# Activations and shared buffers of a two-block transformer kernel moved to multiples of 128 bytes in SBUF

## What is computed

```python
def first_block(x, ...):
    for i in range(2):
        hn = rms_norm(x, norm_mix[i])
        x = x + (even_mixer(hn, ...) if i % 2 == 0 else odd_mixer(hn, ...))
        x = x + sqrelu_mlp(rms_norm(x, norm_mlp[i]), mlp_w1[i], mlp_w2[i])
    return rms_norm(x, norm_final)

def second_block(x, ...):
    h = rms_norm_2(x, mix_norm_pre[layer])
    proj = jnp.einsum("bsd,de->bse", h, w_in[layer])
    ...
    up = jnp.einsum("bsd,df->bsf", rms_norm_2(x, ffn_norm_pre[layer]), w_up[layer])
    ...
    ffn_out = jnp.einsum("bsf,fd->bsd", jax.nn.gelu(gate) * val, w_down[layer])
    return x + rms_norm_2(ffn_out, ffn_norm_post[layer])
```

## The kernel before

| tensor | address before | modulo 128 |
|---|---|---|
| raw, w_lo | 16,512 | 0 |
| w_hi | 57,472 | 0 |
| bias | 98,432 | 0 |
| x | 114,880 | 64 |
| ident, ones | 123,072 and 123,584 | 64 |
| eps_ones | 130,272 | 96 |
| act_hi | 132,800 | 64 |
| act_lo | 140,992 | 64 |
| tmp0 region | 149,184 | 64 |
| arena region | 157,376 | 64 |

## Time and profile before

### The profile page before, as it was taken

How to read it: one execution, slowest core, us unless ns; L and a number is a source line. 1 busy time by engine, 2 the same in 40 slices (tenths; PEclk the granted TensorE clock), 3 DMA queues, 4 the chain that set the end, 5 groups by cost and what they waited for, 6 DMA issues and landing times.

```text
span 1220.7 us, 21634 instructions
## 1 busy us (share of the span) xinstructions
PE 1155.7 (95%) x9407; PEld 1111.2 (91%) x9407; DVE 794.5 (65%) x1131; ACT 587.8 (48%) x824; POOL 147.3 (12%) x83
## 2 busy tenths in 40 slices
PE   6899899999999999999999999999977979999997
PEld 5898679999998999999999989999975879999997
DVE  5647548775546565877543978875554678888842
ACT  4257645444334555444334465663354446665531
POOL 3000012000220003000022201400050030111000
PEclk9699799999999999999999999999988999999999
DMA  9733125655654544565565362555941444566550
GB/s 279 202 114 124 40 66 177 186 194 177 200 177 141 168 141 139 173 190 190 179 200 175 97 210 70 173 161 182 314 137 35 138 139 139 176 198 197 193 187 35
DMA packets 198770, 195.71 MB, mean 160 GB/s; under 512 B 9691, under 2 KB 196756, under 8 KB 198676
## 3 DMA queue, kind: packets, MB, share of 16 engines
q1 hardware_dynamic: 191360, 188.43, 48.6%
q10 hardware_dynamic: 7316, 5.91, 1.9%
HBM read 192.86 MB, written 1.46 MB: 159 GB/s over the span
## 4 chain that ended last, share of the span: by engine, by line
PE 79%; DVE 10%; DMA 3%; ACT 3%; POOL 2%; issue 2%; ACTq 1%; DVEq 0%; POOLq 0%
PE ps_gemm L1561 70%; PE ps_score L1628 2%; PE ps_out L1655 2%; DVE w_lo L1023 2%; PE ps_trans L1640 2%; DMA f_bias<-cum_scr 2%; PE ps_score L1850 2%; DVE prob L1063 1%; POOL f_bias L642 1%; DVE xc L1334 1%; DVE prob L1092 1%; ACTq L778 1%; PE ps_gemm L1726 1%; DVE rs L1035 1%; ACTq L765 1%
## 5 line engine op out<-in xcount | busy, mean ns | idle before, releaser
L1561 PE MATMUL ps_gemm<-act_hi,w_hi 128*128 128x256 f32 x1640 | 463.3, 284 | 19.1 <-ACT act_hi L957 6.7
L1561 PE MATMUL ps_gemm<-act_hi,w_lo 128*128 128x256 f32 x1640 | 458.3, 281 | 0.0
L1561 PE MATMUL ps_gemm<-act_lo,w_hi 128*128 128x256 f32 x1640 | 446.3, 281 | 0.0
L1023 DVE TENSOR_TENSOR w_lo<-raw,w_hi 128x2048 fp32r<-128x2048 f32 (+2 forms) x179 | 408.4, 2290 | 51.4 <-ACT w_hi L683 51.1
L683 ACT ACTIVATE w_hi<-raw 128x2048 fp32r<-128x2048 f32 (+2 forms) x179 | 332.6, 1862 | 187.6 <-DMA raw<-in_mlp_w 97.1
L1561 PEld LDWEIGHTS ps_gemm<-act_hi,w_hi 128*128 128x128 f32 x1640 | 311.2, 190 | 27.6 <-issue 17.5
L1561 PEld LDWEIGHTS ps_gemm<-act_hi,w_lo 128*128 128x128 f32 x1640 | 310.8, 190 | 0.2
L1561 PEld LDWEIGHTS ps_gemm<-act_lo,w_hi 128*128 128x128 f32 x1640 | 302.6, 188 | 1.5
L1561 PE MATMUL ps_gemm<-hid_lo,w_hi 128*128 128x256 f32 x512 | 143.1, 280 | 0.0
L1561 PE MATMUL ps_gemm<-hid_hi,w_lo 128*128 128x256 f32 x512 | 143.1, 280 | 0.0
L1561 PE MATMUL ps_gemm<-hid_hi,w_hi 128*128 128x256 f32 x512 | 142.8, 279 | 0.0
(11 more groups left out here) (282 smaller groups left out, 1733.4 us busy)
## 6 DMA issues: line engine op xcount, KB each, us to landing
raw<-in_mlp_w SPq DMA_DIRECT2D x64, 1024.0 KB, 5.3
raw<-in_w_in SPq DMA_DIRECT2D x30, 1024.0 KB, 5.5
raw<-in_w_up SPq DMA_DIRECT2D x24, 1024.0 KB, 5.3
raw<-in_od_w_in SPq DMA_DIRECT2D x12, 1024.0 KB, 5.1
raw<-in_w_down SPq DMA_DIRECT2D x12, 1024.0 KB, 5.3
raw<-in_ev_w_in SPq DMA_DIRECT2D x9, 1024.0 KB, 6.2
raw<-in_w_proj_a SPq DMA_DIRECT2D x8, 640.0 KB, 4.3
raw<-in_ev_w_out SPq DMA_DIRECT2D x4, 1024.0 KB, 5.5
```

The costliest lines, as they stand in the source:

```text
L1023: dve.tensor_tensor(w_lo[:, slot, 0:k, 0:n], raw[:, slot, 0:k, 0:n], w_hi[:, slot, 0:k, 0:n].bitcast(F32), ALU.subtract).then_inc(w_ready, 1)
L1561: ins = pe.matmul(dst, lhs, rhs, start=(first and opens and i == 0), stop=(last and closes and i + 1 == len(order)), skip_group_check=True)
```

## The change

Two numbers in `build`: `top[0]` is moved on by 64 bytes ahead of `act_hi`, and `tmp0` by a further 128, so everything from `tmp0` on lies 192 bytes further.

```diff
@@ -178,9 +178,10 @@
     rs_o = place("ffn_rs", [P, TB])
     fcq = place("f_cum_q", [P, TB, 16])
     fw = place("conv_f", [P, 4, 2 * NH2])
+    top[0] += 64
     act_hi = place("act_hi", [P, NX, T], F32R)
     act_lo = place("act_lo", [P, NX, T], F32R)
-    tmp0 = top[0]
+    tmp0 = top[0] + 128
     arena = tmp0 + 8 * K
     assert arena + 70 * K <= 229344, arena + 70 * K
```

## The result

The change made the kernel slower by 1.3%: 1,234.9 us (four executions, 1,233.4 to 1,239.8) against 1,220.4 (1,215.6 to 1,222.2) for the kernel before on the same chip, a ratio of 1.0128 with a 95% interval of 1.0102 to 1.0153. The profiled execution took 1,235.1 us, its span 1,233.3. The prediction, no change, was wrong, and the time lies above its range.

A forecast was written before the change was run, and what follows sets the result against it. TensorE, busy 95% of the span, was taken to bound the kernel, its gemm matmuls at 113.3 or 117.8 ns pitch. All terms were taken as 0, so the forecast stayed at the start, 1,221.8 us; range 1,196 to 1,229.

The forecast's parts named there:

- Step (1): Gemm matmuls on TensorE: the remainder modulo 128 at which an operand starts has price 0.
- rival A: Gemm matmuls: distance between the two operands picks the faster level; 15.6 us gain, 31.2 at the end (1,190.6); chance 0.29.
- Rival C: Gemm matmuls: equal remainders make the two operand reads meet; fast stretches fall to slow pitch, 5.4 us slower, 1,227.2; chance 0.22.
- C's mark: Sign in the last stage: it holds 384 matmuls in 45 us instead of 400.
- Rival B: Gemm matmuls: a level below both known pitches, 111.3 ns, reached with equal remainders; 1,174.4 us; chance 0.07.
- Rival D: ident, ones, x and eps_ones stay off multiples of 128; at most +1 us, 1,222.8; counted with no change, together 0.42.
- Step (2): VectorE, ScalarE and GpSimd: price 0 for the moved addresses, ends -0.1 and +0.1 us for the two on the chain.
- Step (3): Pairs pulled apart, such as prob and ident in 156 wide transposes: 0 to +1 us, taken as 0.
- C's tail: Gemm matmuls: a third, slower level for all the slow ones, 31 us more, 1,258; left out of the range with 0.07.

The follow-up runs named there:

- the kernel with distance 112: Against the kernel before, all activations 48 bytes further on (112 from the weights, modulo 256), h2 alone kept at 64: 1,202.2 us, ratio 0.9844.
- the one with distance 96: Against the kernel before, all that the change moved placed 32 bytes further on instead, 96 from the weights modulo 256: 1,237.2 us, ratio 1.0155.
- act alone: Against the kernel before, only act_hi and act_lo 64 bytes further on (128 from the weights); shared buffers stay 64 from them, modulo 256: 1,227.4 us, ratio 1.0060.
- the arena alone: Against the kernel before, only the shared buffers (hid, mix, h2 and others) 192 bytes further on, 0 from the weights modulo 256: 1,230.1 us, ratio 1.0073.
- the small kernel: Computes none of the reference; TensorE alone repeats the gemm's matmuls with operands at many distances: 120.0 ns at 0, 117.8 or 113.3 at 64, 118.7 at 128.

## Why the prediction was wrong

**What bounds the kernel** was right: TensorE's pitch, two levels at full clock, other engines with slack. From the kernel with distance 112 over the kernel before to the one with distance 96, the short pitches sum to 933, 958 and 980 us and the spans are 1,199, 1,221 and 1,232. Between neighbours the clock of an execution counts as much: act alone and the arena alone have 968.5 and 965.6 us of short pitches but spans of 1,226.8 and 1,229.3, at clocks of 0.973 and 0.966.

**Step (1), the price of the remainder, 0.** This failed. The argument was that the two arrangements swap the remainders and show equal levels. That is true, and in the small kernel too the pitch stayed the same when both operands moved by 64. But it says nothing on the distance between them, which was 64 bytes (modulo 256) in every gemm of the trace and becomes 128 and 0. I wrote in rival A that no row excludes this and then priced the step at 0 all the same. A variable that has one value in the whole trace can't be priced from it; the bound for it had to come from outside, and the step should have carried the wide end. The step also worked modulo 128, though the last column of the table of the change shows that modulo 256 the change splits into two different moves. What the runs showed in its place is a price for the distance. Against the slow level it is 0.9 ns a pitch at distance 128 and 2.2 at 0, against the fast one 5.3 and 6.7, and 17.5 us in all.

**The sentence that the level is not a function of the addresses alone** was right (the same program drew both levels at 205 to 360 us in two executions), but I used it against rival A. Addresses decide which levels exist, the start decides between them.

**Rival C** had the right sign and, as far as the runs show it, the right mechanism, a load and a moving stream that disturb each other, and the wrong size. Its term was 1,190 matmuls falling to 117.8 ns, 5.4 us. Measured: all of the 8,180 or so pitches changed, the slow ones too. The third, slower level was in the text, but with the step of 4.5 ns that lies between the two known ones, hence 31 us, and was left to a tail. The step (0.9 and 2.2 ns) and, in the main term, the count (all of them and not 1,190) are the two mis-sized factors. C's mark, 384 matmuls in 45 us of the last stage, reads 377 (50 us held 419).

The Trainium skill (SBUF — State Buffer, section Who interferes with whom) was cited for two independent read ports of TensorE, by which C would cost nothing. The measurement decides against that reading: with the same instructions and nothing beside TensorE, the distance between the two operands alone moved the pitch from 113.3 to 121.7 ns (112 and 116 bytes). The rule of 16-byte lines (section Door 1) fails here too as a reason for equal times: distance 64 and 128 are both whole lines away and differ by 0.9 ns at the slow level and 5.4 at the fast one.

**Rival A** (distance picks the level, faster) had the right variable and the wrong sign for this change. The kernel with distance 112 is that rival come true, at 18 of the 31 us it had as its end. **Rival B** did not come: no stretch of 256-wide matmuls has a mean below 113.3 ns in any run. **Rival D** priced ident and x, which stay where they were, at +1 us at most, and that was right: the 156 transposes of prob took 303 ns each against 304 before, though prob was pulled from ident.

**Step (2)**, the other engines at 0, held: 420 and 419 ns, and 633 against 634 for ScalarE on tensors that moved. But its reasoning for ScalarE was empty. The slope of 0.83 ns was taken from the very two groups whose fixed costs were then found equal, and two points always agree with the line through them. Only the run after tests it. **Step (3)** held: 156 x -1 ns.

**The range** ended at 1,229 because C's tail was cut. With step (1) unpriced, the ends should have been A's 1,190.6 and C's 1,258. Both signs turned out to be real, at different distances. Two readings behind the sums were a little off and change nothing: with the clock of 0.969 the time at half clock is 76 us and not at most 73, and 177 starts stand 200 to 240 ns apart and not some 300.

## What to carry to other kernels

Where loads of the stationary operand and moving streams run back to back, the relative place of the two operands in the partition is a parameter worth 6% of the pitch, and a round address is no better than another: sweep the distance in a small kernel over one period, with several starts and with the operands at the places that they have in the kernel, and take a distance whose value holds at all of them. When an argument from a trace uses symmetry, write down which variables never vary in it; those it cannot price.

Two executions of one unchanged program differed by 0.7% because a long stage fell into another of two pitches at its start. Before explaining a difference of that size, count the matmuls in the same windows of both profiles, and compare their granted clocks: 0.969 and 0.976 on the mean are 17 us more or less at half clock in a span of 1,220.

## What the runs showed of the hardware that I had not expected

- The pitch of 128 x 128 by 256 float32r matmuls with a load each depends on the distance of the operands' starts, and the values at 256, 320, 384, 448 and 512 were those at 0, 64, 128, 192 and 0 to 0.1 ns: 113.3 ns (112; 192 at some starts), 116.7 (32, at most starts), 117.8 (64, at most starts), 118.7 (128, at most starts), 120.0 (0, 96, 108), 121.7 (116). Four bytes either side of 112 cost 6.7 and 8.4 ns.
- It is not the distance alone: both operands moved by 64 bytes left the levels in place, both moved by 16 took distance 112 from 113.3 to 120.0 ns.
- A shorter load is not always a cheaper one: at distance 0, 128 columns ran at 120.0 ns, 64 at 113.3 and 16 at 116.7.
- Two stable levels for one stream exist with nothing running beside TensorE, and a start picks one, within its first dozen matmuls. One stage kept its level for 190 us.
- A faster TensorE waited somewhat more for the others. From 980 to 933 us of short pitches the rest of the span rose from 252 to 265 us. At clocks of 0.976 and 0.970 these two traces have 59 and 72 us at half clock, which can make up to 6.5 of the 13 us; the other half or more is not the clock. Between the kernel before and after the rest fell by 5.0 us although the clock went from 0.969 to 0.967.
